# New item weights for the prompt's second-layer stages in a two-layer hybrid backbone kernel

## What is computed

```
h  = rms_norm(x, norm1_g) * (1 + sc1) + sh1
qa, ka, va, qb, kb, vb, ci, cb, cc = split(h @ w_in)          # 2560 columns
oa = gqa_attention(qa, ka, va)                                # 6 heads of 64
ob = diff_attention(qb, kb, vb, lam)                          # 6 heads, two softmaxes each
oc = short_conv_mixer(ci, cb, cc)
x  = x + g1 * (merge(norm(oa), norm(ob), norm(oc)) @ w_out)
h  = rms_norm(x, norm2_g) * (1 + sc2) + sh2
s  = (h @ peer_wq) against peer_keys                          # 8 heads, two halves, 128 keys each
eidx, gate = the best 16 of the 16 x 16 sums of the two halves' best 16
act = gelu(sum_d u_tab[eidx] * h);   x = x + g2 * sum_k gate * act * v_tab[eidx]
```

## Time and profile before

| | us |
|---|---|
| median of 3 runs | 3009.83 (2999.77 to 3010.87) |
| the profiled execution, whole | 3009.86 |
| its span, first to last instruction | 3008.1 |
| PE busy (DVE, POOL) | 1561.5 (1619.3, 1557.0) |
| mean granted PE clock, of full speed | 0.697 |
| gathers: issues, MB | 1536, 805.40 |

### The profile page before, as it was taken

How to read it: one execution, slowest core, us unless ns; L and a number is a source line. 1 busy time by engine, 2 the same in 40 slices (tenths; PEclk the granted TensorE clock), 3 DMA queues, 4 the chain that set the end, 5 groups by cost and what they waited for, 6 DMA issues and landing times.

```text
span 3008.1 us, 21921 instructions
## 1 busy us (share of the span) xinstructions
PE 1561.5 (52%) x6476; PEld 687.7 (23%) x6476; DVE 1619.3 (54%) x3970; ACT 282.0 (9%) x734; POOL 1557.0 (52%) x1601
## 2 busy tenths in 40 slices
PE   6665757857334443335345584775733334233345
PEld 2334325525201110111123132543510000000001
DVE  1414686653664756454741288655376575766510
ACT  0211003211000000010000001311100000000000
POOL 0002531256667666535565664125667767776665
PEclk8777865678656776657677796578866665656556
DMA  8677992379999999858998986248989999999988
GB/s 283 248 249 255 367 342 71 102 287 386 386 395 401 371 384 405 310 188 326 349 397 336 408 311 246 63 143 313 371 341 387 403 382 391 393 394 381 376 331 336
DMA packets 299015, 963.25 MB, mean 320 GB/s; under 512 B 28280, under 2 KB 30712, under 8 KB 298128
## 3 DMA queue, kind: packets, MB, share of 16 engines
q0 software_dynamic: 221184, 805.40, 70.2%
q1 hardware_dynamic: 77712, 156.44, 14.3%
HBM read 959.12 MB, written 2.62 MB: 320 GB/s over the span
## 4 chain that ended last, share of the span: by engine, by line
DMA 25%; PE 24%; DVE 20%; POOL 15%; issue 14%; ACT 1%; SPq 0%; POOLq 0%; DVEq 0%; ACTq 0%
DMA ring<-peer_v,v_rows 15%; POOL ring L659 14%; DVE ring L1453 9%; PE ps_acc L920 7%; DMA ring<-peer_u,u_rows 6%; PE ps_mm L743 3%; PE ps_mm L797 3%; PE ps_mm L858 2%; PE ps_mm L886 2%; PE ps_mb L823 1%; DMA weights<-w_in 1%; DMA weights<-peer_wq 1%; PE ps_tr L808 1%; DMA weights<-ada_w 1%; PE ps_mb L682 1%
## 5 line engine op out<-in xcount | busy, mean ns | idle before, releaser
L920 PE MATMUL ps_acc<-ring,coef_cols 128*32 128x512 f32 x3072 | 619.3, 948 | 1119.1 <-DMA ring<-peer_v,v_rows 1119.0
L659 POOL DMA_INDIRECT ring<-peer_u,u_rows x768 | 784.8, 1022 | 686.3 <-DVE dots L1453 469.3
L659 POOL DMA_INDIRECT ring<-peer_v,v_rows x768 | 748.6, 975 | 423.0 <-issue 230.7
L1453 DVE CUSTOM_DVE_ANT_0 ring<-ring,ps_tr 128x1024 f32<-128x1024 f32 x512 | 618.0, 1220 | 369.0 <-DMA ring<-peer_u,u_rows 352.1
L920 PEld LDWEIGHTS ps_acc<-ring,coef_cols 128*32 128x32 f32 x3072 | 123.2, 146 | 1539.6 <-issue 1529.0
L1453 DVE CUSTOM_DVE_ANT_0 ring<-ring,h 128x1024 f32<-128x1024 f32 x256 | 307.7, 1223 | 112.1 <-DMA ring<-peer_u,u_rows 98.1
L743 PE MATMUL ps_mm<-weights,hT 128*128 128x512 f32 x480 | 218.8, 615 | 27.0 <-DMA weights<-w_in 22.5
L886 PE MATMUL ps_mm<-hT,weights 128*128 128x128 f32 (+1 forms) x1024 | 201.3, 356 | 21.3 <-DMA weights<-peer_wq 21.3
L886 PEld LDWEIGHTS ps_mm<-hT,weights 128*128 128x128 f32 x1024 | 172.7, 214 | 86.0 <-issue 47.4
L624 POOL TENSOR_SCALAR u_rows<-picks 128x16 uint32<-128x16 f32 x48 | 16.9, 352 | 289.1 <-DVE picks L1426 288.0
L1477 DVE TENSOR_TENSOR h<-h,ps_acc 128x1024 f32<-128x1024 f32 x6 | 7.3, 1221 | 240.9 <-PE ps_acc L920 240.9
(11 more groups left out here) (206 smaller groups left out, 1562.5 us busy)
## 6 DMA issues: line engine op xcount, KB each, us to landing
weights<-ada_w SPq DMA_DIRECT2D x24, 2048.0 KB, 10.2
weights<-w_in SPq DMA_DIRECT2D x20, 2048.0 KB, 14.5
weights<-peer_wq SPq DMA_DIRECT2D x16, 2048.0 KB, 14.3
weights<-w_out SPq DMA_DIRECT2D x8, 2048.0 KB, 14.1
ring<-peer_u,u_rows POOLq DMA_INDIRECT x768, 6.3
ring<-peer_v,v_rows POOLq DMA_INDIRECT x768, 7.0
weights<-peer_keys SPq DMA_DIRECT2D x4, 1024.0 KB, 7.1
par<-params SPq DMA_DIRECT2D x2, 1026.0 KB, 8.0
```

Of the source, the lines that this page charges most:

```text
L659: pool.indirect_dma_start(ring[:, place % RING, :], None, src, bass.IndirectOffsetOnAxis(ap=rows, axis=0)).then_inc(row_full[place % RING] ...
L920: last = pe.matmul(ps_acc[QROWS * k:QROWS * (k + 1), b * NB:(b + 1) * NB], coef_cols[:, i // PART % 2, at:at + QROWS], ring[:, slot("v", n ...
L1453: dve.tensor_tensor_reduce(row, row, h, 1.0, 0.0, ALU.mult, ALU.add, dots[:, n // UNIT % 2, n % UNIT:n % UNIT + 1]).then_inc(u_used, 1)
```

## The change

The weights of steps, until now one table of constants, become a table by kind of step, one for the latents (False) and one for the prompt (True). The latents' values are the old ones (`pq` 10 was 5 times two tiles). The prompt's: norm 4 to 10, projection 20 to 9, qk and keys 2 to 3, tile 4 to 8, head 2 to 7, output 16 to 9, pq 5 as before. The total goes from 264 to 281. The generators yield the kind's name instead of its weight; `Beside` looks the weight up. `chunks()` finds the places of chunks by the kinds; the order of the chunks stays.

```diff
-W_NORM, W_PROJ, W_QK, W_KEYS_T, W_HEAD, W_TILE, W_OUT, W_PQ = 4, 20, 2, 2, 2, 4, 16, 5
...
+WEIGHTS = {False: dict(norm=4, proj=20, qk=2, keys_t=2, tile=4, head=2, out=16, pq=10),
+           True: dict(norm=10, proj=9, qk=3, keys_t=3, tile=8, head=7, out=9, pq=5)}
+
+
+def steps(tiles):
+
+    nt = len(tiles)
+    kinds = ["norm"] * nt
+    kinds += ["proj"] * (IN_CHUNKS * nt) + ["qk"] * (QK_PARTS * nt)
+    kinds += ["keys_t"] * (1 if tiles == P_TILES else 3)
+    kinds += (["tile"] + ["head"] * HEADS + ["tile"]) * nt
+    return kinds + ["out"] * (OUT_CHUNKS * nt) + ["norm"] * nt + ["qk"] + ["pq"] * 16
 
 
 def dense_weight(tiles):
...
+    return sum(WEIGHTS[tiles == P_TILES][kind] for kind in steps(tiles))
...
-            self.done += next(self.program)
+            self.done += self.weights[next(self.program)]
...
-    return Beside(program(), dense_weight(tiles), SPREADS.get(of, UNIT))
+    return Beside(program(), WEIGHTS[tiles == P_TILES], dense_weight(tiles), SPREADS.get(of, UNIT))
...
-                        yield W_HEAD
+                        yield "head"
```

More of the change, by code:

```diff
@@ L122, with __init__ @@
 class Beside:
-    def __init__(self, program, weight, items):
-        self.program, self.weight, self.share = program, weight, weight / items
+    def __init__(self, program, weights, weight, items):
+        self.program, self.weights, self.weight, self.share = program, weights, weight, weight / items
         self.due, self.done = 0.0, 0
@@ L131, in item @@
         while self.done < self.due - 1e-6 and self.done < self.weight:
-            self.done += next(self.program)
+            self.done += self.weights[next(self.program)]
     def end(self):
-        for w in self.program:
-            self.done += w
+        for kind in self.program:
+            self.done += self.weights[kind]
         assert self.done == self.weight, (self.done, self.weight)
 def nothing():
-    return Beside(iter(()), 0, 1)
+    return Beside(iter(()), {}, 0, 1)
 class Segment:
@@ L189, in chunks @@
         for tiles in (P_TILES, S_TILES):
-            nt, nk = len(tiles), 1 if tiles == P_TILES else 3
-            out = nt * (1 + IN_CHUNKS + QK_PARTS + 2 + HEADS) + nk
-            found = [(nt + n * nt, 0, [("in", l, tiles, n)]) for n in range(IN_CHUNKS)]
+            nt, kinds = len(tiles), steps(tiles)
+            proj = [at for at, kind in enumerate(kinds) if kind in ("proj", "late_proj")]
+            out = kinds.index("out")
+            found = [(proj[n * nt], 0, [("in", l, tiles, n)]) for n in range(IN_CHUNKS)]
             found += [(out + n * nt, 0, [("out", l, tiles, n)]) for n in range(OUT_CHUNKS)]
@@ L722, in norm @@
                     last.then_inc(h_mm, 1)
-                    yield W_NORM
+                    yield "norm"
             def dense_stages(l, tiles):
@@ L827, in dense_stages @@
                     scores(0)
-                    yield W_TILE
+                    yield "tile"
                     for head in range(HEADS):
@@ L892, in dense_stages @@
                         half_scores(15)
-                    yield W_PQ * nt
+                    yield "pq"
             def turn(unit):
```

56 lines of the change are left out of this document (27 added, 29 removed).

## The result

The change made the kernel a little slower: 3014.95 us, median of 20 runs (3009.14 to 3025.1), against 3006.61 for the kernel before (20 runs, 2999.18 to 3014.93); ratio 1.0031 [1.0021, 1.004]. That is +8.3 us where -11.7 was forecast. It lies inside the range, but on the other side of no change.

A forecast was written before the change was run, and what follows sets the result against it. Bound: gathers held up in segment 4 by POOL's wait for DVE's dots to free ring slots. Losses of 17.2 + 38.9 + 5.1 less before's 72.9 give -11.7 us, so 2998 us, range 2975 to 3024.

The forecast's parts named there:

- The ring's places by i mod 4: Needed v tile lands 11, 9, 7 or 5 places after item i's u tile, for i mod 4 = 0, 1, 2, 3.
- The projections: Moved to items 7, 14, 21, 27, 34 of segment 3: DVE does not wait in them, so nothing lost.
- Tile start and first head: Segment 3, items 52 and 58: 24.6 us late, then a loop of 18.5; 17.2 lost after the cover.
- The heads at items 5 and 10 of segment 4: PE is there before DVE, under 13 u tiles already gathered: nothing lost; if that fails, up to a loop each.
- six loops, items 15 to 47: Segment 4, head to head: 22.8, 17.9, 15.4 us and the same again, +28.4 over the items' own pace.
- to the tile end, n = 16: Segment 4, last loop, to item 58, 16 tiles to issue: 38.2 us against 28.8, +9.4.
- segment 3 over before: Segment 3 forecast 22.4 us longer: 17.2 lost at tile start and head, 5.2 for two MB of weights.
- segment 5: Output steps at items 0 and 7 cost 2.5 us, second norm at 13 another 2.6: 5.1 lost; segment forecast +7.7.
- the six loops of before: Kernel before, items 27 to 53: loop formula (issue, landing, PE group, chain) held against them, sum stated 11.5 us short.
- The DMA engines hiding short waits: Rival, segments 3 and 4: queued tiles cover short waits, 29 us idle against 56, time 2988; chance 0.35.
- The same loss however the heads lie: Rival: each of eight loops carries the 1.9 us excess, 15 in all, giving +3.5, time 3013; chance 0.12.
- The slower rival: Rival: loops cost 22.4 us at any distance, +14 to +42, 3024 to 3052; decides from 20.3 a loop; chance 0.11.

The follow-up runs named there:

- phase 3: Changed kernel with keys at 49, tile start 51, 12 heads and tile end four items apart, all at i mod 4 = 3: 3077.29 us, 0.9886 of the kernel before.
- phase 0: Changed kernel with heads and tile end four items apart, tile start 52, all at i mod 4 = 0: 3159.92 us, 1.0148 of the kernel before.

## Why the prediction was wrong, and where it was right

**What held.** The bound: the time moves with POOL's wait for dots (16.2 us less in segment 4, the segment 16.1 shorter). The ring's places by i mod 4: phase 3 against phase 0 shows them alone, 2.6%. The projections cost nothing when they alone are moved, within 5 us. Tile start and first head: dots 50 to 58 of segment 3 take 48.4 us; forecast were 24.6 late on top of two items' 5.2, and the loop of 18.5, 48.3 in all. The heads at items 5 and 10 of segment 4 made no wait, and the head at item 0 waits where the two units meet. Timeline of DVE, changed kernel, the maxima at items 58 of segment 3 and 0, 5, 10, 15 of segment 4, after the tile start's first operation:

```profile
1139.61 0.42 DVE L1325 TENSOR_TENSOR merged<-ps_mb,par 128x256 f32<-128x256 f32 x1 [22.55 <-PE ps_mb L785]
...
1162.10 0.29 DVE L1302 TENSOR_REDUCE rowmax<-ps_mm 128x1 f32<-128x128 f32 x1 [9.27 <-PE ps_mm L808]
...
1191.83 0.29 DVE L1302 TENSOR_REDUCE rowmax<-ps_mm 128x1 f32<-128x128 f32 x1 [13.07 <-PE ps_mm L808]
...
1197.99 0.29 DVE L1302 TENSOR_REDUCE rowmax<-ps_mm 128x1 f32<-128x128 f32 x1
...
1206.08 0.28 DVE L1302 TENSOR_REDUCE rowmax<-ps_mm 128x1 f32<-128x128 f32 x1
...
1220.69 0.29 DVE L1302 TENSOR_REDUCE rowmax<-ps_mm 128x1 f32<-128x128 f32 x1 [3.51 <-PE ps_mm L808]
```

The 13.07 is no loss of the head's own as far as can be seen: between the dots of items 63 and 0 lie 16.2 us now and 19.9 before, without a head.

**What failed.** Two things: the size of the loops, and the sharing out of everything that is not a loop. Forecast -11.7, measured +10.1 by the segments of the two traces (+8.3 by the medians), so 21.8 us to explain:

| term | forecast | measured | off |
|---|---|---|---|
| six loops, items 15 to 47 | 112.2 | 124.5 | +12.3 |
| to the tile end, n = 16 | 38.2 | 39.6 | +1.4 |
| segment 3 over before | +22.4 | +28.2 | +5.8 |
| the rest of segment 4 | | | +12.0 |
| segment 5 | +7.7 | -2.0 | -9.7 |

*The loops.* "Loops of n = 8, 4, 2, 8, 4, 2 take 22.8, 17.9, 15.4 and the same again": they took 23.6, 19.9, 19.2, 24.3, 19.2, 18.3. The rows of the changed kernel show where the 12.3 lie. The chains from PE's group to the dot, taken as 3.1 each, are 7.1 too short in all, and 6.0 of that stands in the two loops with n = 2, where the chain took 6.3 and 6.0 us (1280.36 to 1286.63, and 1342.37 to 1348.33): DVE's routing. The run with routing one item earlier takes it away: 15.3 and 15.4 us there. I had the routing in the rows: the 3.4 us chain of a mixer B head was taken as 3.1 "as some routing lies in it", and the six loops of before were found short and "six further stages lie inside". I counted which stages shift and never asked which items DVE's routing pieces fall on. They repeat every 16 items, and so, by accident, do the new heads (15, 31, 47). The landings are 4.0 of the 12.3: the six took 6.61, 6.29, 5.97, 6.07, 6.53 and 5.3, mean 6.1, and 0.14 us more each until PE starts. The last 1.1 is POOL's pitch and PE's group. The 5.6 was no bad middle for the kernel before, whose six have a mean of 5.5; that they would grow was not foreseen, and why they do is open. The figure cited from the Trainium skill (DMA: Bandwidth & Descriptors, Anatomy of one DMA), an estimate of 4.1 us with POOL's part, lay further off in the same direction; the trace, with 4.98 to 6.61 us, decides against it.

A slip in the working: for the last two loops of before, the prediction's own terms give 23.3 us each and not 22.8 and 22.9, so the formula was 10.5 us short over the six, 1.8 a loop. And "most of the 40 slices" at 370 GB/s or more are 18 of the 40.

*Segment 3* did not miss where the tile start and the head are, which came out at 48.4 for 48.3. It missed before them: items 14 to 50 take 109.1 us where they took 95.9, 13.2 more for 5.2 of weights. The run with the projections alone has 11.6 more there, and gets 4.8 back behind item 50, where the fourth projection used to stand; in the changed kernel the tile start takes that place. Whether the projections cost something together with it, as they do not alone, was not run.

*The rest of segment 4.* Dot 15 came 3.8 us later than before, where 11.3 was counted. From the tile end to unit 5's first dot there are 42.6 us; before's end, 45.4 us for five items more, would leave 32.3. And the 7.8 taken off for 3 MB of weights hardly shows where it can be seen alone: the projections' run has 2 MB fewer and is 0.8 us shorter. If none of it comes, the three make 10.6 of the 12.0. The weights leave a segment whose DMA engines idle anyway (share 0.79) and go where the share is 0.99, so the time need not move along with the bytes, as the prediction had it. These are readings of single traces, and no run parts the three.

*Segment 5.* Most of its -9.7 is a matter of where the segments are cut. The first output step now stands before unit 5's first dot (DVE waits 10.5 us there) and the second was behind it before (8.4 us at item 2), so that wait is now counted in segment 4, as part of the 42.6; the forecast had it in segment 5. Taken together, item 63 to 5:2 is 3.5 us shorter than before, where 2.5 longer was forecast, and 5:2 to 5:20 is 9.6 longer, where 2.6 was: +6.1 for the 5.1. The sum of this term is near by luck, since neither part is right. The second norm at i mod 4 = 1 waits on this (chain, changed kernel):

```profile
1443.60 10.96 DMA ring<-peer_v,v_rows
1454.69 3.64 PE ps_acc L931 x16
1458.34 2.51 PE ps_mb L693 x4
```

A landing of 10.96 us stands in it, twice the 5.6, and it is no accident: the other two traces of the changed kernel have 10.46 and 10.44 at this place. In the kernel before the one in front of this norm took 6.41. What lies beside it is SP's loading of two `peer_wq` chunks, changed kernel, then before:

```profile
1436.27 32.05 SPq L569 DMA_DIRECT2D weights<-peer_wq  x2
```

```profile
1427.70 30.66 SPq L558 DMA_DIRECT2D weights<-peer_wq  x2
```

They start 8.6 us later now, and the v tile is issued 7.3 us behind their start, not 11.2. The prediction let weights cost bytes only; that they hold this gather up is likely, but no run shows it.

**The rivals.** The DMA engines hiding short waits (2988) fell: segment 4 shrank by POOL's own sum of waits, and by the shares the DMA engines idled some 64 us in segments 3 and 4 (0.09 of 210.1 and 0.19 of 238.2) where they had idled 55; the rival had the idle time fall to 29. The same loss however the heads lie (3013) has the time about right and the reason wrong: its 1.9 us a loop is what was found (12.3 over six, 2.1), but mostly by named causes, and the loss does depend on where the heads lie, by 82 us. The reading that went with it, that the repeating gap can mean too few buffers (the Trainium skill, Perfetto Trace Analysis, Optimization Strategy), is not enough here: with the same 14 slots POOL's u gathers wait 81.3 or 23.5 us in segment 4 by phase alone. What more slots would bring was not run. The slower rival said that it decides from 20.3 us a loop on, where the sum equals before; the loops were 20.75 in the mean. Its mechanism, a loop that costs the same at any distance, is not so: 23.6 at n = 8 and 15.3 at n = 2 once the routing is out of the way. Its threshold was the more useful number than my 0.11 for it. The test "unit 5's first dot after 1410" called it: 1430.5. POOL's wait for dots was to be near 40 us in segment 4 and came to 63.4, and 17 more in segment 3 came to 23.

**What spreading the heads was worth.** The heads' new items lie on all phases; the old ones lay on all phases too, only closer. The tile start went from the best phase (item 27) to the worst (item 52). Neither table of weights looks at i mod 4.

**Open.** Whether the change costs less on the slower chip (1.0005) than on the first kind (1.0031 and 1.0018): the intervals just overlap; the 24 us wait of the first run with earlier routing; why the landings grew. Each trace is one execution.

## What to carry to other kernels

Where an engine executes waiting stages in line with the work that frees a ring, the phase of the wait against the groups in which the producer works can count more than the stages' spacing (2.6% against 0.3% here): write the places down modulo the group and put every wait just before the producer's next group, as far behind the last one as it goes. Just behind a group is the worst place, since that group's last tile was issued last. List all that the waiting engine does at those items, also what the change does not touch, since work with a period of its own lands between the wait's end and the freeing of the slot. When a forecast stands a few us from a rival's break-even, and the formula is short on every loop it was held against, put the shortfall into the sum. And ask of weights that move not only how many bytes they are, but whether the place they leave and the place they come to wait for transfers.

## What the runs showed of the hardware

The same program ran 3.4 and 3.5% longer on two chips than on a third (3111.64 and 3113.78 against 3008.96 for the kernel before), and gathers are slower where they run alone: units 8 and 7 side by side take 177.36 us at 393 GB/s on the first, and on the second of the slower ones, kernel before:

```profile
2255.10:2445.90 190.80, 59.26 (x260) 11.92 (x260) 113.10 (x274) 1.42 (x6) 127.88 (x139) 0.56 0.97 366
```

7% less bandwidth at a DMA share still near 1, for the same bytes. The granted clock of PE is lower there too (0.56 against 0.64), but PE is busy for 59.26 of the 190.80 us and does not set the pace. A loop made of latencies and one made of bandwidth may then weigh differently, so a change that trades the one for the other need not show the same ratio on both.
